# Reordering the opening and the last retention head of a two-layer decoder step

## The reference

```
mod   = silu(c) @ w_ada + b_ada ;  shift, scale, gate = split(mod, 3)
h     = rmsnorm(x, g) * (1 + scale) + shift
layer 0 (retention, 4 heads, dk 256, dv 512, chunks of 128):
  q, k, v, g = split(h @ w_ret_in)
  scores = (q k^T) * decay ; o = scores v + (q * q_decay) S_old
  S_new  = chunk_decay * S_old + (k * k_decay)^T v
  x = x + gate * ((layernorm(o) * silu(g)) @ w_ret_out)
layer 1 (block-sparse attention over pages of a K/V cache): the same frame with another mixer
```

## Time and profile before

| | |
|---|---|
| median of 3 runs | 668.54 us (667.92 to 669.15) |
| the profiled execution | 667.59 us, of which the span is 665.8 us |
| PE busy | 620.9 us, 93% |
| DVE, ACT, POOL busy | 56%, 35%, 34% |
| DMA | 190.28 MB, mean 286 GB/s |
| mean granted TensorE clock | 0.971 |

### The profile page before, as it was taken

The page is one execution under the profiler, slowest core; times in us unless marked ns, Lnnn a source line. Parts: engine busy times, 40 slices in busy tenths (PEclk is TensorE's granted clock), DMA queues, the critical chain, the costliest instruction groups (busy, mean ns, idle before and its releaser), DMA issues. The chain is left out here.

```text
span 665.8 us, 11278 instructions
## 1 busy us (share of the span) xinstructions
PE 620.9 (93%) x4285; PEld 383.1 (58%) x4285; DVE 373.3 (56%) x718; ACT 231.4 (35%) x475; POOL 223.4 (34%) x239
## 2 busy tenths in 40 slices
PE   5789999999999999989999999999999998878996
PEld 4547646664666466643566756767744456443542
DVE  3333837483748374835543743335798875774723
ACT  4245232523252326214043515555134145341010
POOL 0051228022802280223176148999920012020000
PEclk9989999999999999989999999999999989797999
DMA  8997374887587748894796573344999999999993
GB/s 306 377 389 270 127 253 170 305 315 252 181 320 288 253 151 321 319 354 154 266 338 230 206 244 143 127 158 146 392 349 403 410 408 407 409 401 408 402 369 111
DMA packets 82193, 190.28 MB, mean 286 GB/s; under 512 B 4119, under 2 KB 12583, under 8 KB 82012
## 3 DMA queue, kind: packets, MB, share of 16 engines
q1 hardware_dynamic: 80484, 183.70, 74.4%
q0 software_dynamic: 1120, 4.46, 1.9%
q10 hardware_dynamic: 536, 1.41, 0.6%
HBM read 167.14 MB, written 22.41 MB: 285 GB/s over the span
## 5 line engine op out<-in xcount | busy, mean ns | idle before, releaser
L534 POOL TENSOR_TENSOR weights_low<-ring,weights_high 128x512 fp32r<-128x512 f32 x96 | 124.0, 1339 | 79.5 <-PE bank L781 43.1
L1352 ACT ACTIVATE weights_high<-ring 128x1024 fp32r<-128x1024 f32 x84 | 86.4, 1054 | 103.2 <-PE bank L800 78.6
L792 PE MATMUL bank<-weights_high,h_high 128*128 128x512 f32 x272 | 109.7, 403 | 0.0
L792 PE MATMUL bank<-weights_high,h_low 128*128 128x512 f32 x272 | 107.2, 394 | 0.0
L800 PE MATMUL bank<-weights_low,h_high 128*128 128x512 f32 x272 | 82.3, 401 | 0.9 <-DVE weights_low L534 0.9
L792 PEld LDWEIGHTS bank<-weights_high,h_high 128*128 128x128 f32 x272 | 51.4, 189 | 26.4 <-issue 15.1
L534 DVE TENSOR_TENSOR weights_low<-ring,weights_high 128x512 fp32r<-128x512 f32 x72 | 44.8, 686 | 27.8 <-PE bank L781 16.4
L800 PEld LDWEIGHTS bank<-weights_low,h_high 128*128 128x128 f32 x272 | 50.0, 188 | 14.3 <-DVE weights_low L534 3.9
L792 PEld LDWEIGHTS bank<-weights_high,h_low 128*128 128x128 f32 x272 | 51.4, 189 | 11.1
L1870 DVE TENSOR_TENSOR partial_low<-bank,partial_high 128x512 fp32r<-128x512 f32 x26 | 17.9, 688 | 67.6 <-ACT partial_high L1303 38.8
L1667 POOL TENSOR_TENSOR keys_by_sequence<-key_parts,consts 128x2048 fp32r<-128x2048 f32 x4 | 15.1, 3765 | 111.2 <-DVE key_parts L1965 111.2
(11 more groups left out here) (257 smaller groups left out, 1009.8 us busy)
## 6 DMA issues: line engine op xcount, KB each, us to landing
ring<-in_w_ada SPq DMA_DIRECT2D x12, 2048.0 KB, 12.8
ring<-in_cache_k SPq DMA_DIRECT2D x40, 512.0 KB, 10.5
ring<-in_cache_v SPq DMA_DIRECT2D x40, 512.0 KB, 9.5
ring<-in_w_ret_in SPq DMA_DIRECT2D x8, 2048.0 KB, 10.6
ring<-in_state_ret SPq DMA_DIRECT2D x32, 512.0 KB, 8.4
out_state_sample<-ring SPq DMA_DIRECT2D x32, 512.0 KB, 6.2
ring<-in_w_moba_in SPq DMA_DIRECT2D x8, 2048.0 KB, 8.7
arena<-in_cache_k SPq DMA_DIRECT2D x24, 512.0 KB, 10.4
```

The costliest lines, as they stand in the source:

```text
L534: tensor_tensor(w_low[:, slot, k, :], ring[:, slot, k * CH:(k + 1) * CH], high[:, k, :].bitcast(F32), ALU.subtract).then_inc(low_ready[LOW ...
L792: pe.matmul(o[i][:, :], xs[p][i][:, k, :], high[:, k, :], start=k == 0 and p == 0, stop=False)
L1352: nc.scalar.activation(w_high[u[0] == "moba"][:, 2 * i:2 * i + 2, :].rearrange("p a b -> p (a b)"), w[:, 2 * i * CH:(2 * i + 2) * CH], ACT ...
```

## The change

In the opening, chunk `ADA_FIRST[1]` is moved ahead of the second halves of `x_turned`, and chunk `ADA_FIRST[2]` ahead of the sample rows' `x_turned`. Each `part_turned` gets other PE work between it and the `ada_part` it needs. Three `keep_busy` calls of 3, 3 and 5 products into bank 4 are new. ACT copies chunk `ADA_FIRST[2]` before it rounds the first halves of `h`, and DVE turns it before it subtracts them.

In the last head, the scores come ahead of both gate chunks, and the old-state products stand between `choices(0, 4)` and `choices(0, 5)`. DVE scales the scores first and takes the modulation afterwards. The bank of `("part", "o", 3)` becomes 5, and that of `("row", "o", 3, 2)` becomes 4.

```diff
@@ PE, opening
-            for n in range(2):
-                x_turned(0, n, 1)
+            ada_part(0, ADA_FIRST[1])
+            x_turned(0, 0, 1)
+            part_turned(0, ADA_FIRST[1])
+            x_turned(0, 1, 1)
+            ada_part(0, ADA_FIRST[2])
             x_turned(0, 2, 0)
-            for c in ADA_FIRST[1:]:
-                ada_part(0, c)
-                part_turned(0, c)
+            part_turned(0, ADA_FIRST[2])
+            keep_busy(bank[4], 3)
+            ada_part(0, ADA_FIRST[3])
+            keep_busy(bank[4], 3)
+            part_turned(0, ADA_FIRST[3])
+            keep_busy(bank[4], 5)
             pe.wait_ge(sample_h, 1)
@@ PE, head loop
                 ada_part(1, ADA_FIRST[h])
-                if h in ADA_AT:
-                    ada_part(0, ADA_GATE[0])
-                    part_turned(1, ADA_FIRST[h])
-                    ada_part(0, ADA_GATE[1])
-                    choices(0, ADA_GATE[0])
-                    choices(0, ADA_GATE[1])
                 o = open_bank(("scores", h))
...
-                if h not in ADA_AT:
+                if h in ADA_AT:
+                    ada_part(0, ADA_GATE[0])
+                    part_turned(1, ADA_FIRST[h])
+                    ada_part(0, ADA_GATE[1])
+                    choices(0, ADA_GATE[0])
+                else:
                     part_turned(1, ADA_FIRST[h])
...
                 sealed(last, ("part", "o", h))
+                if h in ADA_AT:
+                    choices(0, ADA_GATE[1])
@@ ACT, opening
             copy_part(("ada", 0, ADA_FIRST[1]))
+            copy_part(("ada", 0, ADA_FIRST[2]))
             h_rounded(0, 0, 0, 0)
             h_rounded(0, 1, 0, 1)
-            copy_part(("ada", 0, ADA_FIRST[2]))
             copy_part(("ada", 0, ADA_FIRST[3]))
@@ DVE, opening
             h_scaled(0, 0, 0)
             h_scaled(0, 1, 0)
+            modulation_turned(0, ADA_FIRST[2])
             h_left(0, 0, 0, 0)
             h_left(0, 1, 0, 1)
-            modulation_turned(0, ADA_FIRST[2])
@@ DVE, head loop (the modulation of the last head moves behind the scaling of its scores)
-                if h in ADA_AT:
-                    modulation_turned(1, ADA_FIRST[h])
-                for layer, c in ADA_AT.get(h, ()):
-                    modulation(layer, (c,))
                 o = wait_full(dve, ("scores", h))
...
-                if h not in ADA_AT:
-                    modulation_turned(1, ADA_FIRST[h])
+                modulation_turned(1, ADA_FIRST[h])
+                for layer, c in ADA_AT.get(h, ()):
+                    modulation(layer, (c,))
```

More of the change, by code:

```diff
@@ L222, in bank_plan @@
         use(("part", "ada", 1, ADA_FIRST[h]), 4)
+        misc(("scores", h))
+        misc(("mT", 1, ADA_FIRST[h]))
         if h in ADA_AT:
-            misc(("mT", 1, ADA_FIRST[h]))
             ada(0, ADA_GATE)
-        misc(("scores", h))
-        if h not in ADA_AT:
-            misc(("mT", 1, ADA_FIRST[h]))
-        use(("part", "o", h), 4)
+        use(("part", "o", h), 5 if h in ADA_AT else 4)
         pair(("row", "o", h, 0), ("row", "o", h, 1))
-        use(("row", "o", h, 2), 5)
+        use(("row", "o", h, 2), 4 if h in ADA_AT else 5)
         misc(("S", h, 0))
```

## The result

The changed kernel takes 663.77 us (median of 6 runs, 662.96 to 665.26) against 668.36 us (6 runs, 666.25 to 669.15). The ratio is 0.9938, with a 95% interval of 0.9912 to 0.9965. That is 4.1 us faster by the ratio (4.6 by the difference of the two medians), where 8.2 were forecast: the sign is right and the size is half. The time itself lies inside the stated range of 658.4 to 664.0, near its slow end. The profiled execution took 665.26 us, with a span of 663.5 us. It is the slowest of the six, so the comparison of spans (665.8 to 663.5) shows only 2.3 us. The lines of the changed kernel are moved by a few: PE's sample product is L780 in place of L781, `ada_part` L859 in place of L860, `add_groups` L681 in place of L682, the prompt state L1039 in place of L1031, the output projection's first sample part L690 in place of L691.

The account below looks back on a forecast made before the run. Loads bind in the opening and page stage, PE in between. Opening 3.0 us and last head 5.2 sum to 8.2, so 668.54 becomes 660.3 for the median (659.4 for the profiled execution); range 658.4 to 664.0.

Parts of the forecast that it names:

- a broadcast that holds up the weights: Rival, opening: POOL's broadcast delays the weights by 2.2 us, or the clock stays low; opening gives 1 us, 662.3; chance 0.17.
- losses behind 466 us: Rival, page stage: part of the gain is given back behind 466 us; half lost gives 664.4 us; chance 0.07.
- The opening: First projection starts at 36.9 and its sums at 50.4; gain 3.3 less 0.3, 3.0 us, bounds 0.8 and 3.5.
- The floor: Opening: the first weights' second half lands at 36.8 us, unmoved by the change; the first projection can't start before 36.9.
- The broadcast: Opening: POOL's 1 MB broadcast is issued 2.2 us before the weights land and delays them; 0.3 us taken.
- I leaned to full clock: Opening, first projection: full clock puts its sums at 50.4, gain 3.3 us; with the clock as now 51.6, gain 2.1.
- The last head: PE's waits and half-clock stretch go; prompt state starts 5.7 us earlier; net gain 5.2 us, bounds 4.2 and 5.7.
- What could be late next: Last head: ACT and DVE work stays hidden, old states cost 0 to 0.5 us, layer norm starts 0.3 later.
- behind it every stage as long as before: Sign to look for in the changed kernel's profile: stages after the last head keep their lengths.
- the term of 0.3 behind the head: Behind the last head: DVE's layer norm starts some 0.3 us later relative to PE, delaying what waits for DVE.
- The rival of slow output tiles: Rival, end: output tiles at 1.2 GHz cost up to 7.1 us more each; two make it 674.5; chance 0.02.
- One small sum of the prediction: Last head: states and first rout unit, 16.6 us of loads behind 284, land at 300.9, due at 306.3.

Follow-up runs that it names:

- e2: The kernel before with only the last head's part of the change, banks as changed; 665.71 us against 666.71, ratio 0.9968.
- e4: The kernel before with only the swap of banks 4 and 5 in the last head; 668.96 us against 666.71, ratio 1.0018.
- e6: e1 with the sample rows' and the second prompt tile's x_turned exchanged in the opening; 660.27 us against 668.07 for the kernel before, ratio 0.9901.
- e9: e1 with the exchange of e6 and the idle products of e7; 660.71 us against 666.27 for the kernel before, ratio 0.9911.
- e3: The kernel before with only the opening's part of the change, on PE, ACT and DVE; 662.77 us against 666.71, ratio 0.9929.
- e5: e1 without the eleven idle products of the opening; 662.83 us against 668.07 for the kernel before, ratio 0.9936.
- e11: The changed kernel, unaltered, measured and profiled a second time; 663.10 us against 666.27 for the kernel before, ratio 0.9941.
- e10: e1 measured again, on one chip with e9 and e11; 660.98 us against 666.27 for the kernel before, ratio 0.9924.
- e1: The changed kernel with the old banks in the last head; 661.17 us against 666.71 for the kernel before, ratio 0.9892.
- e7: e1 with seven idle products in PE's last two waits for DVE; 661.47 us against 668.07 for the kernel before, ratio 0.9914.

## Why the prediction was half right

That the time fell inside the range is luck: the slow end of the range was meant for a broadcast that holds up the weights and for losses behind 466 us, and neither is what cost the time.

**The opening: right.** Forecast 3.0 us, L780 at 36.9, L681 at 50.4. Over the profiles the mean of L681 is 53.87 with the old order (before, e2, e4) and 50.95 with the new one and its idle products (seven profiles, e6 and e9 left out), a gain of 2.9. The floor was the landing of the weights, and the last step before L681 was POOL: in the changed kernel PE waits 0.23 us there for `weights_low`. In the changed kernel's own profile the sample rows (ready at 37.5) were later than the weights (landed at 37.0), since the fourth chunk ran at half clock; that is most of the 0.7 us between 37.60 and 36.9. The broadcast, for which I took 0.3 us and to which a rival gave 2.2, shows no cost: 0.2 us between e3 and the kernel before, less than the 0.5 by which the landing differs among the profiles in which it was issued later. The Trainium skill (DMA: Bandwidth & Descriptors, section Queues, rings and completion order) has the queues with work take turns packet by packet. An issue 1.9 us ahead of the landing (e3) shows no loss from it: the weights landed at 37.0.

**The clock in the opening: right for the first projection, wrong for the chunk ahead of it.** I leaned to full clock because the wait would be short, "with more work before it". What decides it is the idle products: in all nine profiles that have them the first sample product takes 1.92 us, in all four that don't (before, e2, e4, e5) 2.85 to 3.64, and e5 has the new order. That the fourth chunk itself could run at half clock, as in three of seven profiles, the prediction didn't consider.

**The last head: the mechanism right, the gain sized against a slow base.** From the start of the chunk ahead of the scores to the prompt state the forecast has 17.7 and 1.8, 19.5 us; the changed kernel has 19.94. Forecast gain 5.7 less 0.2, measured 5.2 against the earlier trace rows. But the earlier trace rows were of an execution in which the clock stayed low for 7 us. The same order takes 23.65 in e3 and 23.71 in e4, against 25.14: behind the same wait of 1.86 us the clock fell in these too, but for some 3.4 us. In the ten profiles with the new order it stays at full through the head. The mean of the three is 24.2, that of the ten profiles with the new order 20.0: the gain is 4.1 on average, where 5.5 were forecast ahead of the layer norm's 0.3. This may also be why e3 by its time gains more than its opening, but one profile doesn't show it for its other runs.

**What could be late next: wrong.** This is the step that failed. The prediction says that DVE's layer norm starts "some 0.3 us later relative to PE, and what waits for DVE behind the head comes later by that". Its sign "behind it every stage as long as before" failed there: 29.16 us against 25.78. It followed data and loads, and said nothing of the banks: it didn't ask who opens bank 4 next. The diff in the bank plan was two numbers and was described as a detail; it put PE's first work behind the head after DVE's last reading. Price: 1.3 us of wait net, and 1.6 more of slow clock in one of the three changed-order profiles with that wait unfilled (changed; not e2 and e11). So the term of 0.3 behind the head measured 3.4 us in the changed kernel's profile (29.16 less 25.78) and 1.7 in e2 and e11. The layer norm's own part of it was 0.45, which is 26.23 less 25.78, from the profiles with the old banks.

**Behind 466 us: no loss is shown, and one isn't excluded.** The page stretch is 321.2 to 322.3 in eleven profiles and 323.9 and 324.2 in e5 and e11, for which I found no cause; the changed kernel's 322.11 against 321.79 is within that. The rival of slow output tiles didn't come: the last of them (L1159 before, L1167 in the changed kernel) takes 7.11 us in every profile. What came in small is a fall of the clock at the last sample products, 1.6 us in seven of the eleven profiles without idle products there: in one of three with the old order of the last head (e4), in six of eight with the new one. That is too few to say whether the change makes it likelier.

**The sum.** 2.9 and 4.1 less 0.45, 1.3 and a third of 1.6 gives 4.7 us. Of the 3.5 that lack to the forecast's 8.2, the bank is 1.8, the slow base 1.4, the layer norm and the opening 0.1 to 0.2 each. The changed kernel was measured 4.1 us faster by its ratio, and 3.9 in e11; the 0.6 to 0.8 between are within the intervals and not explained. With the old banks it is 2.9 and 4.1 less 0.45, 6.6 us, between the 5.1 and 7.2 measured in e10 and e1. The versions with the old banks and the idle products, e1 (and e10), e6, e7 and e9, lie at 0.989 to 0.992 of the kernel before and can't be told from each other by time.

One small sum of the prediction is off without effect: 284 and 16.6 is 300.6, not 300.9, and both are well ahead of 306.3.

## What to carry to other kernels

When a diff changes which buffer a result goes into, follow that buffer to its next user, past the end of the block that was changed: here two numbers in a plan cost 1.8 us of the 6.6 that the new order gains without them. And a base that holds a stretch at the lower clock is one draw: look in a second execution of it how long the slow stretch lasts before its removal is counted as a gain.

## What the runs showed of the hardware

In all nine profiles with the eleven idle products in three waits of the opening, the first sample product took 1.92 us, at 2.4 GHz. In all four without them (before, e2, e4, e5) it took 2.85 to 3.64. In e5 and e2 the granted clock was at full until 37.9 and 38.1 and fell within 0.3 us of the start of that product (37.80 and 38.33), behind a wait of 1.20 and 1.28 us, with a wait of 0.8 us for ACT ahead of that. I had not expected that waits so short could come before a fall. They need not bring one: behind the wait of 1.96 and 1.97 us before L690 the clock stayed at full in e2 and e11 and fell in the changed kernel.

The idle products don't keep the clock up everywhere. The same kernel differs from execution to execution in where it falls: with the order of the change the fourth chunk took 1.92 us in four profiles and 2.90 to 3.41 in three, and in those three the clock was back at full ahead of the first projection. In the changed kernel it fell at about 30.6 us although PE had been busy from 25.57 without a gap, with products of 32 columns from 27.42 to 30.1. Such falls cost 0.7 to 1.6 us each here, as much as an edit of this kind is worth.
